# Part of the second feed-forward product by Strassen's seven products

## The chip, the cores and the metric

One Trainium2 chip, one core of it. The metric is the device time of one execution in microseconds (us). The kernel's inputs and outputs are in HBM; the matrix engine (TensorE, PE in the rows), VectorE (DVE), ScalarE (ACT), GpSimd (POOL) and the engine that issues the weight transfers (SP) each take their instructions in order and meet at semaphores.

## The reference, cut to what matters

Two layers (DEPTH = 2) over 640 tokens (128 context, 512 latent) with 1024 channels. A layer normalises, runs three token mixers, projects and gates them ("the mix"), applies an output projection, and then the feed-forward part that this change is about:

```
h2 = rms_norm(x, norm2_g) * (1 + scale2) + shift2
x  = x + gate2 * (square(relu(h2 @ w_ff1)) @ w_ff2)      # 1024 -> 4096 -> 1024, all fp32
```

## The kernel before, in words

**Layout.** Channels lie on the 128 partitions, tokens along the free axis, in two halves of 320 columns. A weight tile is 1024 input channels by 128 output channels, 8 rows of 128x128 (k = 0 to 7). An fp32 product is made from two fp32r parts: ScalarE casts the high part (`cast_entry`, L1278 and L1274), VectorE subtracts it from the full value to get the low part (`low_entry`, L1687), and TensorE does three matmuls (hi*hi, hi*lo, lo*hi) for each row and half. A whole tile takes 8 x 2 x 3 = 48 matmuls of 320 columns.

**Weights.** SP loads tiles in a fixed order into 4 places (`raw`); a place is loaded again when its low parts are made. The high and low parts go through a ring of 4 entries of 4 rows each (`ENTRIES`, `place`). Entry r+4 may be cast when TensorE has used entry r, so the casts stand two tiles or four blocks ahead in ScalarE's and VectorE's queues.

**Feed-forward.** The 4096 hidden channels go in 4 blocks (`FF_BLOCKS`), f = 0 to 3. In a block, 8 hidden tiles are computed (first product), then 8 output tiles from those 8 (second product), each added to `x` with its gate (`add_to_x`, L1885). A hidden tile passes relu and square on ScalarE (L1287, L1289), its cast (L1291, `hid_hi`) and its low part on VectorE (`hid_low`, L1687). `hid` has two buffers, for tile q mod 2, and so has `gqk`, the product before relu.

**Sevens.** Most first products are done in pairs of tiles by Strassen's seven products (`pair_by_sevens`, L894). The 2 x 2 blocks are rows 0 to 3 and 4 to 7 of the weights by the two tiles, and the same rows by the two token halves of h. A pair takes 7 blocks of 4 x 3 = 12 matmuls, 84 for 96. GpSimd makes four sums of weight quarters for it (`block_sums`, L672 to L680; 128x512 each), VectorE combines the results (L1720 to L1732), ScalarE copies three of them (L1300). The four combinations of h are made once, when h is new (`make_diff` L1764, `low_diff`). In block 0 tiles 0 to 3 are whole and 4 to 7 by sevens; in blocks 1 to 3 all are by sevens. The second products are all whole. The pair of tiles q and q+1 is called "pair q" here; the seven blocks, their ring entries and the steps (n) are counted from 0.

**Order.** Each engine's order is written out by hand. In `pair_by_sevens` VectorE does at step n: one result sum, the low part of the entry four ahead, and at some n the low part of a hidden tile. ScalarE does at step n a copy and the cast of the entry four ahead; after step 1 it treats hidden tile q-1, and after step 6 hidden tile q.

**Mix.** The first of 8 mix steps (m = 0) has two whole gate tiles and one whole projection tile, the others use sevens. ScalarE's sigmoids there come ahead of the casts of the next weight tiles.

Of the kernel before, what the change touches and what calls it, by code (L numbers as in the profile page):

```python
# [119 lines left out]

def by_sevens(s):

    i = s % PER
    if MIX0 <= i < OUT0:
        m, q = divmod(i - MIX0, 3)
        return m >= 1 and q < 2
    f, q = divmod(i - FF0, 2 * KT)
    return f >= 0 and q in (range(4, KT) if f == 0 else range(KT))
# [7 lines left out]

def in_mix(s):
    return MIX0 <= s % PER < OUT0


def plain(s):

    return sum(not by_sevens(t) for t in range(s + 1))


def ring_entries():

    out = []
    for s in range(MAIN):
        if leads(s):  # L150
            out += [(s, n, False) for n in range(SEVEN)]
        elif not by_sevens(s):
            out += [(s, n, True) for n in range(2)]
# [4 lines left out]
RING = {s: r for r, (s, n, whole) in enumerate(ENTRIES) if n == 0}  # L158
LEADERS = [s for s in range(MAIN) if leads(s)]
BLOCK = {s: SEVEN * n for n, s in enumerate(LEADERS)}  # L160
# [3 lines left out]
def whole_product(o):  # L164
# [4 lines left out]
    return o < O_FF or not by_sevens(FF0 + o - O_FF)  # L169


def done(o):

    return sum(whole_product(n) for n in range(o + 1)) + (KT if o >= O_MIX else 0)


def blocks_until(s):

    return BLOCK[s] + 6 if leads(s) else BLOCK[s - 1] + 7

# [4 lines left out]
def product_of(s, half):  # L185
# [7 lines left out]
    else:  # L193
        n = done(O_OUT + (i - OUT0))
# [95 lines left out]
def build(nc, xT, cond, first, stream, small, vecs, table, dft, mask, yT, ckvT_out, krT_out, st_out, x_kept):  # L290
# [9 lines left out]
    with ExitStack() as ctx:  # L300
# [143 lines left out]
        p57_sb = sem("p57_sb")  # L444
        mix_sig = sem("mix_sig", 2 * (KT - 1))
# [209 lines left out]
        def _(pool):  # L655
# [6 lines left out]

            def block_sums(s):
# [6 lines left out]
                if b > 0:  # L670
                    pool.wait_ge(block_lo, b - SEVEN + 3)
# [18 lines left out]
            for e.layer in range(DEPTH):  # L690
# [43 lines left out]
        def _(pe):  # L734
# [139 lines left out]
            def pair_by_sevens(o, i, free):  # L874
# [24 lines left out]
                modulation(i + 1)  # L899

# [33 lines left out]
            for e.layer in range(DEPTH):  # L934
# [291 lines left out]
                for f in range(FF_BLOCKS):  # L1226
                    i, o = FF0 + 2 * KT * f, O_FF + 2 * KT * f
                    for q in range(4 if f == 0 else 0):
# [7 lines left out]
                    for q in range(4 if f == 0 else 0, KT, 2):  # L1236
                        n = o + q
                        first = q == (4 if f == 0 else 0)
                        pair_by_sevens(n, i + q, {0: n - 2, 2: n - 1} if first else {0: n - 4, 2: n - 2, 3: n - 1})
# [1124 lines left out]
```

## Time and profile before

| what | value |
|---|---|
| median of 3 runs | 2067.82 us (2067.37 to 2068.98) |
| the profiled execution's own time | 2063.75 us |
| its span, first to last instruction | 2062.0 us |
| mean granted TensorE clock | 0.992 |
| TensorE busy | 1980.4 us, 96% |
| VectorE / ScalarE / GpSimd busy | 59% / 46% / 14% |
| chain that ended last | TensorE 82%, VectorE 11%, ScalarE 3% |

A matmul's row shows its time through the pipeline (309 ns); the next one starts before it ends, so rates are read from start times. "Idle before" is the time an engine sat before an instruction, with what ended it. The chain goes back from the last instruction to what released each step.

### The profile page before, as it was taken

How to read it: one execution, taken by the hardware profiler on the slowest of the kernel's cores; microseconds unless marked ns; L12 is line 12 of the kernel's file. 1: busy time of each engine (PE TensorE's matmuls, PEld its weight loads, DVE VectorE, ACT ScalarE, POOL GpSimd, SP SyncE). 2: the span in 40 equal slices, each digit the busy share in tenths (PEclk: the TensorE clock that was granted, in tenths of full speed). 3: DMA queues.
4: the chain of work that ended last, by engine and by line, in shares of the span. 5: the costliest groups of instructions: out<-in, count | busy, mean ns of one | idle time of the engine just before them, and what ended most of it. 6: DMA issues, size and time to landing. Idle time of an engine off the chain costs nothing.

```text
span 2062.0 us, 34108 instructions
## 1 busy us (share of the span) xinstructions
PE 1980.4 (96%) x13976; PEld 1810.8 (88%) x13976; DVE 1217.4 (59%) x2095; ACT 946.0 (46%) x1746; POOL 284.7 (14%) x229
## 2 busy tenths in 40 slices
PE   6999999999999999999999999999999899999997
PEld 3995688899888999999989866888999899999997
DVE  4245688756468273736553466877664764646464
ACT  5535544534366161625454355453442743535262
POOL 1000000222012130403100000003220312121210
PEclk9999999999999999999999999999999999999999
DMA  9210001343523324242432100113443121213221
GB/s 367 74 51 11 1 27 52 114 166 128 188 81 112 144 91 150 68 149 88 158 109 74 36 6 1 47 58 120 163 162 124 51 89 65 94 62 103 62 94 60
DMA packets 53035, 195.92 MB, mean 95 GB/s; under 512 B 6032, under 2 KB 8144, under 8 KB 52112
## 3 DMA queue, kind: packets, MB, share of 16 engines
q1 hardware_dynamic: 49408, 174.61, 25.2%
q0 software_dynamic: 3472, 19.14, 2.6%
q8 instruction: 111, 1.82, 0.4%
q14 instruction: 44, 0.36, 0.1%
HBM read 187.79 MB, written 5.93 MB: 94 GB/s over the span
## 4 chain that ended last, share of the span: by engine, by line
PE 82%; DVE 11%; ACT 3%; issue 2%; DMA 2%; SPq 0%; ACTq 0%; DVEq 0%
PE ps L742 36%; PE ps L894 23%; PE ps L809 2%; PE ps L914 2%; PE ps L1060 2%; PE ps L923 2%; DVE w_lo_parts L1687 2%; PE ps L760 2%; PE ps L1036 2%; PE ps L847 2%; PE ps L1090 2%; PE ps L1065 1%; ACT scratch L1508 1%; DVE scratch L2095 1%; DVE merged L1764 1%
## 5 line engine op out<-in xcount | busy, mean ns | idle before, releaser
L1687 DVE TENSOR_TENSOR w_lo_parts<-w_raw,w_hi_parts 128x512 fp32r<-128x512 f32 x548 | 403.9, 756 | 242.9 <-ACT w_hi_parts L1274 148.2
L1274 ACT CAST w_hi_parts<-w_raw 128x512 fp32r<-128x512 f32 x296 | 172.1, 619 | 457.5 <-PE ps L742 413.4
L742 PE MATMUL ps<-hid_hi_parts,w_hi_parts 128*128 128x320 f32 x1216 | 280.3, 312 | 2.3 <-DVE merged L2154 1.6
L742 PE MATMUL ps<-hid_lo_parts,w_hi_parts 128*128 128x320 f32 x1216 | 277.0, 309 | 0.0
L742 PE MATMUL ps<-hid_hi_parts,w_lo_parts 128*128 128x320 f32 x1216 | 276.9, 309 | 0.0
L1885 DVE SCALAR_TENSOR_TENSOR x<-ps,modulation,x 128x128 f32<-128x128 f32 (+2 forms) x216 | 81.7, 434 | 319.0 <-PE ps L742 319.0
L742 PEld LDWEIGHTS ps<-hid_hi_parts,w_hi_parts 128*128 128x128 f32 x1216 | 201.9, 188 | 25.3 <-issue 22.1
L1278 ACT CAST w_hi_parts<-w_raw 128x512 fp32r<-128x512 f32 x252 | 152.2, 621 | 137.5 <-PE ps L742 56.7
L742 PEld LDWEIGHTS ps<-hid_lo_parts,w_hi_parts 128*128 128x128 f32 x1216 | 203.3, 188 | 0.0
L742 PEld LDWEIGHTS ps<-hid_hi_parts,w_lo_parts 128*128 128x128 f32 x1216 | 203.3, 188 | 0.0
L894 PE MATMUL ps<-h_hi_parts,w_hi_parts 128*128 128x320 f32 x560 | 173.8, 310 | 0.0
L894 PE MATMUL ps<-h_hi_parts,w_lo_parts 128*128 128x320 f32 x560 | 173.0, 309 | 0.0
L894 PE MATMUL ps<-h_lo_parts,w_hi_parts 128*128 128x320 f32 x560 | 172.7, 309 | 0.0
L894 PE MATMUL ps<-diff_hi_parts_a,w_hi_parts 128*128 128x320 f32 x504 | 156.3, 310 | 7.5 <-DVE w_lo_parts L1687 6.3
L742 PE MATMUL ps<-h_hi_parts,w_hi_parts 128*128 128x320 f32 x640 | 148.6, 313 | 0.0
L742 PE MATMUL ps<-h_hi_parts,w_lo_parts 128*128 128x320 f32 x640 | 145.8, 309 | 0.0
L742 PE MATMUL ps<-h_lo_parts,w_hi_parts 128*128 128x320 f32 x640 | 145.7, 309 | 0.0
L894 PE MATMUL ps<-diff_lo_parts,w_hi_parts 128*128 128x320 f32 x448 | 138.3, 309 | 0.0
L742 PEld LDWEIGHTS ps<-h_hi_parts,w_hi_parts 128*128 128x128 f32 x640 | 106.5, 188 | 11.6 <-issue 10.1
L742 PEld LDWEIGHTS ps<-h_hi_parts,w_lo_parts 128*128 128x128 f32 x640 | 107.0, 188 | 0.0
L742 PEld LDWEIGHTS ps<-h_lo_parts,w_hi_parts 128*128 128x128 f32 x640 | 106.9, 188 | 0.0
L894 PEld LDWEIGHTS ps<-h_hi_parts,w_hi_parts 128*128 128x128 f32 x560 | 105.1, 188 | 1.7 <-issue 1.7
(334 smaller groups left out, 4080.9 us busy)
## 6 DMA issues: line engine op xcount, KB each, us to landing
w_raw<-in_stream SPq DMA_DIRECT2D x312, 512.0 KB, 3.9
scratch<-in_first SPq DMA_DIRECT2D x10, 512.0 KB, 14.3
small_weights<-in_small POOLq DMA_DIRECT2D x2, 2048.0 KB, 10.5
h_scratch<-in_first SPq DMA_DIRECT2D x6, 512.0 KB, 17.3
x<-in_xT POOLq DMA_DIRECT2D x2, 1280.0 KB, 11.8
x<-in_xT POOLq DMA_DIRECT2D x8, 320.0 KB, 4.1
x_kept<-x POOLq DMA_DIRECT2D x8, 320.0 KB, 2.5
x<-x_kept POOLq DMA_DIRECT2D x8, 320.0 KB, 4.1
```

Of the source, the lines that this page charges most:

```text
L742: ins = mm(out[:, h, :], weight(w, s, k), a[:, k, h * HALF:(h + 1) * HALF], start=(first and n == 0), stop=(last and n == 2))
L760: last = mm(pair(o)[:, h, :], weight(w, s, k), a[:, k, half_cols(h)], start=(k == 0 and n == 0), stop=(k == KT - 1 and n == 2))
L809: last = mm(pair(o)[:, h, :], weight(w, s, k), a[:, k, half_cols(h)], start=(k == 0 and n == 0), stop=(k == KT - 1 and n == 2))
L847: last = mm(ps[cols:cols + 32, unit_bank(u), :], cs[:, 2 * j + i, :], tiles[i][:, 4 * P * c:4 * P * (c + 1)], start=(j == 0), stop=(j == U ...
L894: last = mm(ps[:, block_bank(s, n), 0:HALF], place(w, RING[s] + n)[:, k, :], a[:, k, :], start=(n < 4 and k == 0 and c == 0), stop=(k == K ...
L914: last = mm(ps[:, 7 - h, 0:HALF], weight(w, s, k), a[:, k, h * HALF:(h + 1) * HALF], start=(k == 0 and j == 0), stop=(k == KT - 1 and j == 2))
L923: return nc.tensor.transpose(out, src, tab(C_ID))
L1036: last = mm(out, sm[:, w:w + P], cq[:, t, CTX:TOK] if j < 4 else cq[:, t, 0:CTX], start=(t == 0), stop=(t == 1))
L1274: copy(place(wh, r), raw_half(s, n)).then_inc(w_hi, 1)
L1278: copy(place(wh, r), block_source(s, n)).then_inc(block_hi, 1)
L1687: return tt(dst, full, hi.bitcast(F32), ALU.subtract)
L1885: ins = stt(x[:, k, cols], src, modv[:, gate * KT + k, g:g + 1], x[:, k, cols], ALU.mult, ALU.add)
```

## The change

Twelve pairs of second-product tiles are done "by parts": `part_pairs(l, f)` gives pairs 0, 2, 4, 6 for the second layer's blocks 1 and 2, and pairs 0 and 2 for block 3. For block 3 the function does not ask for the layer, so the first layer's block 3 is done so too. In such a pair rows 0 to 3 of the contraction are done by seven products (the 2 x 2 blocks are now rows 0, 1 and rows 2, 3), 7 blocks of 2 x 3 = 6 matmuls; rows 4 to 7 are done whole into the same PSUM banks, 48 matmuls. The pair takes 90 matmuls.

- Four combinations of hidden tiles 0 to 3 are needed. VectorE makes them in `hid_differences` (128x640 each, and one copy) during pairs 2 and 4 of the first product, ScalarE casts them (`cast_hid_diff`) in pairs 4 and 6, VectorE makes their low parts (`low_hid_diff`) in pair 6.
- Since they read the two `hid` buffers, `hid_low(q-1)` moves from step 2 to step 5 in pairs 2 and 4 of these blocks, and ScalarE's square of tile q waits there for `hid_low(q-1)` in place of `hid_low(q-2)`.
- In all pairs by sevens ScalarE treats hidden tile q ahead of the cast of step 6, no longer after it. Tile 7 is treated inside the first pair by parts.
- GpSimd makes four half-size weight sums for each pair by parts (`part_sums`). The result is summed in `gqk`, and VectorE adds it to `x` from there.
- In the second layer block 0 does tiles 4 and 5 whole, and only pair 6 by sevens (`first_seven`).
- In the mix's first step ScalarE's casts come ahead of the sigmoids, and VectorE's low parts of two differences move one product later.

```diff
+def first_seven(l, f):
+    return 0 if f > 0 else 4 if l == 0 else 6
+def part_pairs(l, f):
+    if f == FF_BLOCKS - 1:
+        return range(0, 4, 2)
+    return range(0, KT if l == DEPTH - 1 and f > 0 else 0, 2)
...
+            def part_sums(s):
+                s1, s3 = s1_sb[0][:, 0:2, :], s1_sb[0][:, 2:4, :]
...
+                nc.gpsimd.tensor_tensor(s1, a21, a22, ALU.add).then_inc(part_sum, 1)
+                nc.gpsimd.tensor_tensor(s3, a11, a21, ALU.subtract).then_inc(part_sum, 1)
+                pool.wait_ge(part_lo, PIECES * PART[s] + 1)
...
+            def pair_in_parts(f, q, o):
...
+                block(0, 0, 0)
+                pe.wait_ge(hid_ready, e.at(hid_ready, KT * f + 4))
+                block(1, 0, 2)
+                piece_ready(1)
+                lower(b[1], 1, 0, range(4, 6), False)
+                piece_ready(2)
+                read(n - 2)
+                diff_made(1)
+                block(2, 2, 0)
...
+                block(3, 2, 2)
+                lower(b[1], 1, 0, range(6, KT), False)
+                pe.wait_ge(part_copied, 3 * no + 2)
+                lower(b[2], 1, 1, range(4, KT), False).then_inc(part_mm, 1)
...
             def hid_by_sevens(f, q, o):
...
-                act.wait_ge(hid_ready, e.at(hid_ready, KT * f + q - 1))
+                act.wait_ge(hid_ready, e.at(hid_ready, KT * f + (q if q in (2, 4) and (e.layer, f) in DIFFS else q - 1)))
...
             def pair_by_sevens(f, q, o, first):
                 for n in range(SEVEN):
+                    if n == SEVEN - 1:
+                        hid_by_sevens(f, q, o)
                     pair_step(e.layer * PER + FF0 + 2 * KT * f + q, n)
                     if n == 1 and not first:
                         hid_by_sevens(f, q - 1, o)
-                hid_by_sevens(f, q, o)
+                    if (e.layer, f) in DIFFS and (q, n) in ((4, 4), (4, 5), (6, 4), (6, 5)):
+                        cast_hid_diff(f, {(4, 4): 0, (4, 5): 1, (6, 4): 2, (6, 5): 3}[q, n])
...
+            def hid_differences(f, q, n):
+                b1, b2 = hid[:, :, half_cols(0)], hid[:, :, half_cols(1)]
...
+                if (q, n) == (2, 3):
+                    tt(hid_full(0), b2, b1, ALU.subtract).then_inc(hid_diff, 1)
+                if (q, n) == (2, 4):
+                    e.link(cp(hid_full(1), b2))
+                if (q, n) == (4, 3):
+                    tt(hid_full(1), b2, hid_full(1), ALU.subtract).then_inc(hid_diff, 1)
+                if (q, n) == (4, 4):
+                    tt(hid_full(2), b2, hid_full(0), ALU.subtract).then_inc(hid_diff, 1)
+                if (q, n) == (4, 5):
...
+                    tt(hid_full(3), b1, hid_full(2), ALU.subtract).then_inc(hid_diff, 1)
...
                     if n == 0 and not first:
                         hid_low(f, q - 2)
-                    if n == 2 and not first:
+                    parts = (e.layer, f) in DIFFS
+                    if parts and q in (2, 4):
+                        hid_differences(f, q, n)
+                    if n == (5 if parts and q in (2, 4) else 2) and not first:
                         hid_low(f, q - 1)
+                    if n >= 3 and parts and q == KT - 2:
+                        low_hid_diff(f, n - 3)
...
-                    if m == 0:
-                        first_gate(0)
                     for q in range(2 if m == 0 else 0):
                         act.wait_ge(mm_done, e.at(mm_done, done(o + q)))
+                        split_next(i + q)
+                        if q == 0:
+                            first_gate(0)
                         fn(halves(G[:, 1 + q, :]), pair(o + q), ACT.Sigmoid).then_inc(pair_free[(o + q) % 2], 1)
-                        split_next(i + q)
...
-                            for n in ((1, 2), (3,), ())[b]:
+                            for n in ((1,), (2,), (3,))[b]:
                                 low_diff(True, n)
```

## Rows read from the trace of the kernel before

**Rows 1.** The page, part 1: busy time by engine.

```profile
PE 1980.4 (96%) x13976; PEld 1810.8 (88%) x13976; DVE 1217.4 (59%) x2095; ACT 946.0 (46%) x1746; POOL 284.7 (14%) x229
```

**Rows 2.** Timeline (start us, us, what) of TensorE, layer 2, block 1.

```profile
1731.45 0.31 PE L894 MATMUL ps<-h_hi_parts,w_hi_parts 128*128 128x320 f32 x1
...
1780.72 0.46 PE L742 MATMUL ps<-hid_hi_parts,w_hi_parts 128*128 128x320 f32 x2
```

**Rows 3.** ScalarE's timeline, pair 4: relu, square, cast, weight casts.

```profile
1756.81 0.74 ACT L1287 ACTIVATE gla_q_k<-gla_q_k 128x640 f32<-128x640 f32 x1
1757.58 0.74 ACT L1289 ACTIVATE gla_r<-gla_q_k 128x640 f32<-128x640 f32 x1
1758.35 0.73 ACT L1291 CAST hid_hi_parts<-gla_r 128x640 fp32r<-128x640 f32 x1
...
1759.30 1.14 ACT L1278 CAST w_hi_parts<-w_raw 128x512 fp32r<-128x512 f32 x2
```

**Rows 4.** VectorE's timeline, pairs 4 and 6.

```profile
1742.51 0.48 DVE L1725 TENSOR_TENSOR gla_q_k<-ps,low_rank_latents 128x320 f32<-128x320 f32 x1
...
1757.94 1.70 DVE L1687 TENSOR_TENSOR w_lo_parts<-w_raw,w_hi_parts 128x512 fp32r<-128x512 f32 x1
1759.96 1.40 DVE L1687 TENSOR_TENSOR w_lo_parts<-w_raw,w_hi_parts 128x512 fp32r<-128x512 f32 x1 [0.32 <-ACT w_hi_parts L1278]
...
1762.41 0.68 DVE L1687 TENSOR_TENSOR w_lo_parts<-w_raw,w_hi_parts 128x512 fp32r<-128x512 f32 x1
...
1766.45 1.38 DVE L1687 TENSOR_TENSOR w_lo_parts<-w_raw,w_hi_parts 128x512 fp32r<-128x512 f32 x1 [0.54 <-ACT w_hi_parts L1278]
1767.76 0.48 DVE L1732 TENSOR_TENSOR gla_q_k<-low_rank_latents 128x320 f32<-128x320 f32 x1
```

**Rows 5.** GpSimd's timeline over the same time: the weight sums.

```profile
1742.27 1.48 POOL L680 TENSOR_TENSOR w_raw<-w_raw 128x512 f32<-128x512 f32 x1 [0.80 <-DVE w_lo_parts L1687]
...
1757.79 1.31 POOL L672 TENSOR_TENSOR low_rank_latents<-w_raw 128x512 f32<-128x512 f32 x1 [0.72 <-DVE w_lo_parts L1687]
1759.17 1.63 POOL L674 TENSOR_TENSOR w_raw<-w_raw 128x512 f32<-128x512 f32 x1
1765.99 1.29 POOL L677 TENSOR_TENSOR w_raw<-low_rank_latents,w_raw 128x512 f32<-128x512 f32 x1 [5.19 <-DVE w_lo_parts L1687]
1767.91 1.48 POOL L680 TENSOR_TENSOR w_raw<-w_raw 128x512 f32<-128x512 f32 x1 [0.63 <-DVE w_lo_parts L1687]
```

**Rows 6.** VectorE's timeline after pair 6: the last hidden tile's low part.

```profile
1785.92 0.82 DVE L1687 TENSOR_TENSOR hid_lo_parts<-gla_r,hid_hi_parts 128x640 fp32r<-128x640 f32 x1 [1.35 <-ACT hid_hi_parts L1291]
```

**Rows 7.** VectorE's timeline, layer 2, block 0: two differences of 1280 elements.

```profile
1642.29 5.08 DVE L1764 TENSOR_TENSOR merged<-merged 128x1280 f32<-128x1280 f32 x2
```

**Rows 8.** What TensorE waited for from 1560 to 1660 us.

```profile
PE ps L894 <- DVE w_lo_parts L1687: 4.1, 2, 2.4
PE ps L809 <- DVE h_lo_parts L1844: 2.8, 3, 1.8
PE ps L894 <- DVE diff_lo_parts L1687: 1.2, 1, 1.2
```

**Rows 9.** TensorE's timeline, first pairs of the branch mix, both layers.

```profile
376.29 0.56 PE L742 MATMUL ps<-hid_hi_parts,w_hi_parts 128*128 128x320 f32 x2 [1.58 <-DVE merged L2154]
...
385.46 0.41 PE L894 MATMUL ps<-mix_hi_parts_b,w_hi_parts 128*128 128x320 f32 x1 [1.56 <-DVE w_lo_parts L1687]
...
1403.84 0.41 PE L894 MATMUL ps<-mix_hi_parts_b,w_hi_parts 128*128 128x320 f32 x1 [2.66 <-DVE w_lo_parts L1687]
```

**Rows 10.** ScalarE and VectorE at the start of layer 2's mix.

```profile
1382.37 1.28 ACT L1324 ACT_TABLE_LOAD   x1 [0.99 <-DVEq L2124]
...
1384.90 1.13 ACT L1274 CAST w_hi_parts<-w_raw 128x512 fp32r<-128x512 f32 x2
...
1385.54 1.29 DVE L1687 TENSOR_TENSOR w_lo_parts<-w_raw,w_hi_parts 128x512 fp32r<-128x512 f32 x2 [3.30 <-ACT w_hi_parts L1274]
```

**Rows 11.** Window: length; PE, PEld, DVE, ACT, POOL busy; PEclk, DMA share, GB/s.

```profile
1616.00:1620.00 4.00, 3.03 (x13) 3.03 (x14) 3.13 (x9) 2.94 (x8) 0.00 (x0) 0.70 0.42 135
```

More of the change, by code:

```diff
@@ L134, in leads, with leads_parts, whole_tile @@
     return by_sevens(s) and ((i - MIX0) % 3 == 0 if i < OUT0 else (i - FF0) % 2 == 0)
+def leads_parts(s):
+    return by_parts(s) and (s % PER - FF0) % 2 == 0
 def in_mix(s):
     return MIX0 <= s % PER < OUT0
+def whole_tile(s):
+    return not by_sevens(s) and not by_parts(s)
 def plain(s):
-    return sum(not by_sevens(t) for t in range(s + 1))
+    return sum(whole_tile(t) for t in range(s + 1))
+PIECES = 6
+STEPS = 10
+USED_UP = (2, 5, 4, 7, 8, 10)
 def ring_entries():
@@ L150, in ring_entries, with whole_product @@
         if leads(s):
-            out += [(s, n, False) for n in range(SEVEN)]
-        elif not by_sevens(s):
-            out += [(s, n, True) for n in range(2)]
+            out += [(s, n, "block") for n in range(SEVEN)]
+        elif leads_parts(s):
+            out += [(s, n, "piece") for n in range(PIECES)]
+        elif whole_tile(s):
+            out += [(s, n, "half") for n in range(2)]
     return out
 ENTRIES = ring_entries()
-RING = {s: r for r, (s, n, whole) in enumerate(ENTRIES) if n == 0}
-LEADERS = [s for s in range(MAIN) if leads(s)]
-BLOCK = {s: SEVEN * n for n, s in enumerate(LEADERS)}
+RING = {s: r for r, (s, n, kind) in enumerate(ENTRIES) if n == 0}
+LEADERS = [s for s in range(MAIN) if leads(s) or leads_parts(s)]
+AHEAD = dict(zip(LEADERS[1:], LEADERS))
+BLOCK = {s: SEVEN * n for n, s in enumerate(filter(leads, LEADERS))}
+PART = {s: n for n, s in enumerate(filter(leads_parts, LEADERS))}
 PLAIN = [plain(s) for s in range(MAIN)]
-def whole_product(o):
+def whole_product(o, l):
     if O_MIX <= o < O_OUT:
@@ L193, in product_of @@
     else:
-        n = done(O_OUT + (i - OUT0))
+        n = done(O_OUT + (i - OUT0), l)
     return l * DONE + n
@@ L640, in _ @@
                         sp.wait_ge(block_lo, blocks_until(i))
+                    elif was == "main" and by_parts(i):
+                        sp.wait_ge(part_lo, pieces_until(i))
                     elif was == "main":
@@ L1227, in _ @@
                     i, o = FF0 + 2 * KT * f, O_FF + 2 * KT * f
-                    for q in range(4 if f == 0 else 0):
+                    for q in range(first_seven(e.layer, f)):
                         if q == 0:
@@ L1235, in _ @@
                         modulation(i + q)
[L1236 removed]
+                    for q in range(first_seven(e.layer, f), KT, 2):
                         n = o + q
[L1238 to L1240 removed]
+                        first = q == (first_seven(e.layer, f))
+                        pair_by_sevens(n, i + q, {0: n - 2, 2: n - 1} if first and (e.layer, f - 1) not in DIFFS else {0: n - 3, 2: n - 2, 3: n - 1})
+                    for q in part_pairs(e.layer, f):
+                        pair_in_parts(f, q, o)
+                    for q in whole_second(e.layer, f):
                         tile_ready(i + KT + q)
@@ L1692, in low_entry @@
                     return
-                s, n, whole = ENTRIES[r]
-                if whole:
+                s, n, kind = ENTRIES[r]
+                if kind == "half":
                     dve.wait_ge(w_hi, 2 * PLAIN[s] - 1 + n)
@@ L2187, in _ @@
                     i, o = FF0 + 2 * KT * f, O_FF + 2 * KT * f
-                    for q in range(4 if f == 0 else 0):
+                    for q in range(first_seven(e.layer, f)):
                         split_next(i + q)
```

283 lines of the change are left out of this document (244 added, 39 removed).

## The prediction, made before the changed kernel ran

> **What bounds the kernel now.** I read four views. The page first: TensorE is busy 96% of the span, ScalarE, VectorE and GpSimd far less [rows 1]. Then TensorE's start times: the four pairs by sevens of a block are 4 x 84 = 336 matmuls from 1731.45 to 1780.72, so 49.27 us, 0.1466 us each and no gap [rows 2]. A block of 12 matmuls takes 1.76 us, a pair 12.31, a whole tile 7.04. In the feed-forward blocks TensorE alone sets the pace, so removed matmuls count in full as long as its operands stay ahead. Then the waits of TensorE, for places where they don't: block 0 of layer 2 and the first steps of the mix [rows 8, 9]. Last the timelines of the engines that make the operands [rows 3 to 6]: averages over a layer say that VectorE has room, but the change puts its new work in pairs 2, 4 and 6, and there I have to look.
>
> **What VectorE's timeline shows.** A low part of 512 elements takes 0.68 us (two of them 1.29, so 0.60 from start to start) [rows 4, 10], one of 640 takes 0.82 [rows 6]. But the one begun at 1757.94 takes 1.70: GpSimd's sum runs from 1757.79 to 1759.10, and the low part ends 0.54 later. The next sum, issued at 1759.17, takes 1.63 for 1.30, and the low part of 1759.96 ends 0.56 after it. The same at 1766.45 [rows 4, 5]. So an instruction of VectorE with both inputs in SBUF and one of GpSimd don't run together: one waits until the other is through. A result sum that reads PSUM (1742.51, 0.48 us) runs at full speed inside a GpSimd sum (1742.27 to 1743.75) [rows 4, 5]. Differences pay too: two of 1280 elements took 5.08 us, where 0.82 for 640 gives some 3.1 [rows 6, 7].
>
> The Trainium skill says this as a rule ("SBUF — State Buffer", section "Who interferes with whom"): a VectorE instruction with two SBUF inputs contends with a GpSimd one that reads SBUF, and the loser blocks in full. The trace agrees (1.70 us for 0.68), and by this rule the new differences will block as well.
>
> Per pair by sevens SBUF work is now: seven low parts x 0.60 = 4.2, two hidden low parts x 0.74 (0.82 less what overlaps) = 1.5, L1732 0.4, four sums of GpSimd x 1.30 = 5.2; together 11.3 of 12.31 us. The new work must fit into 1.0 us.
>
> **Part 1, matmuls of the twelve pairs.** 90 for 96, so 12 x 6 x 0.1466 = 10.6 us less.
>
> **Part 2, new waits in the four blocks that feed them.** New on VectorE: one difference and a copy in pair 2 (0.74 + 0.45, the copy an estimate), three differences in pair 4 (2.2), four low parts in pair 6 (3.0). In pair 4 that makes 13.5 us of SBUF work for 12.31. But the order costs more than the sum. I walked the four queues forward in order, with start-to-start times from the rows: ScalarE's relu and square 0.77 each, casts 0.63 (hidden) and 0.52 (weights) [rows 3], copies 0.33 (estimate: half of a 640), VectorE as above with 0.40 for a result sum (0.48 less the overlap), and the exclusion of GpSimd. I chose 0.2 us from a block's last matmul to its reader and 0.1 for other semaphores so that the walk fits the code before. There it gives L1732 at 1767.73 and the last `hid_low` at 1785.88; the rows have 1767.76 and 1785.92 [rows 4, 6], and no wait of TensorE, as in the trace. The same walk of the new code, pair 4, counted from TensorE's start of it (it arrives with ScalarE some 1 us late from pair 2):
>
> - VectorE: `p57` sum ends at 10.5, low part of pair 6's entry 0 at 11.1, difference 1 at 11.8. Now GpSimd's L677 has the port: low part of entry 1 ends at 13.6, L1732 14.0. L680 next: difference 2 ends at 15.9. Result sum 16.3, low part of entry 2 16.9, difference 3 17.7, then the next pair's first sum, so `hid_low(3)` ends at 18.9.
> - ScalarE's square of tile 4 waits for that `hid_low(3)` (it waited for tile 2's before): 19.0 to 19.8, its cast to 20.4, and behind it in the queue the cast of entry 3 to 20.9. Its low part is ready at 21.8.
> - Pair 6's block 3 needs entry 3 at 18.8. TensorE waits 3.0.
>
> In pair 2 the same chain (one difference, copy, `hid_low(1)`, square of tile 2, cast, low part) ends 0.9 late for pair 4. In pair 6, 0.3 for entry 2 and 0.2 for `p57`. The first pair by parts starts (call it 0) with VectorE behind: entry 2 is 0.8 late, the bank of block 3 0.2. Hidden tile 6 gets its relu only at 2.8, its low part stands behind the low part of entry 3 and the fourth difference and is ready at 7.8; without further waits row 6 of the lower product would start at 4.4 + 1.0: 2.4 late. Tile 7 comes at 8.9, row 7 0.7 later than its turn. Before, the last low part was ready 6.0 us after the second product's start (1785.92 + 0.82 - 1780.72) and first used after 42 matmuls, 6.2 us [rows 2, 6]; now it is asked for after 33, 4.8 us.
>
> Sum for a block: 0.9 + 0.3 + 3.0 + 0.2 + 0.8 + 0.2 + 2.4 + 0.7 = 8.5 us, four blocks 34, and 0.3 where a block follows a block by parts. From there on the pairs by parts run free: a pair needs 5.5 low parts, half-size sums of GpSimd (0.65, half of 1.30), and some 5 us of sums and additions in 13.2 us; the cast of entry 5 (its place is free at 7.0, needed at 9.7) has 1.3 us to spare. Bounds per block: if the new instructions didn't exclude GpSimd's, 5.3; if nothing did, 3.3 (the relu chain of tiles 6 and 7 alone); with a few tenths more at each of the nine handovers, 10.5. I take 8.5, since the exclusion stands in the rows for the same kind of instruction. GpSimd's new sums and ScalarE's eight-odd new casts are priced by this walk. SP's loads are still released by low parts a whole pair ahead of their casts.
>
> **Part 3, block 0 of layer 2.** 12 matmuls more, +1.8. TensorE waits there 4.1 + 1.2 = 5.3 us for low parts [rows 8], because the differences of h (5.08 for two) stand ahead of them [rows 7]. With two more whole tiles (14 us) these are made before pair 6 needs them (entries 0 and 1 ready some 5 us early), so -5.3. Net -3.5; bounds -3.5 and +1.8 (nothing saved).
>
> **Part 4, the mix.** ScalarE's casts stood behind a table load, a gate and a sigmoid: 1382.37 to 1384.90, and VectorE sat idle 3.3 us for them [rows 10]. They move some 3 us forward, and one low part of 1.5 us leaves the way of entry 3. The waits of the two first pairs are 1.6 + 1.6 + 2.7 = 5.8 [rows 9]. Walking it, block 3 comes in time and block 4 then waits some 1 us in each layer: -3.5. Bounds 0 and -5.8.
>
> **Sum.** -10.6 + 34.3 + 1.8 - 5.3 - 3.5 = +16.7. The profiled execution took 2063.75 us with a span of 2062.0, so it would be 2080.5; the median of the runs shown lies 4.1 above that execution, and the forecast is against the median: 2067.8 + 16.7 = 2084.5. Within 0.2% (4.1 us) I call it the same.
>
> **Rivals.**
> - A, faster: the differences find gaps. For it, VectorE is busy 59% and ScalarE 46% [rows 1]; against it the 11.3 of 12.31 us. With no new waits the sum is -17.6 (2050.2); it stays faster by over 0.2% as long as a block costs under 3.4 us (-17.6 + 4 x 3.4 = -4.1). The lower bound, no exclusion at all, is 3.3. Likeliest time within it 2060. Chance 0.12.
> - B, the same: the new instructions don't exclude GpSimd's, 5.3 a block: -17.6 + 21.2 = +3.6, 2071. Chance 0.10. Speaks against it: rows 7.
> - C, slower still: the waits lower TensorE's clock. After the waits of 2.8 us ahead of 1617 [rows 8] the granted clock was 0.70 of full speed over a window of 4 us [rows 11], 0.30 x 4 = 1.2 us lost. One or two such falls a block are 4.8 to 9.6 us: 2089 to 2094, 2091 taken. Against it: TensorE works 25 us and more without a gap ahead of the first long wait. Chance 0.13.
> - The forecast, 8 to 9 us a block: 0.65, own range 2077 to 2091.
>
> The change does what it says, and layer 1's block 3 more; were that one not by parts, the sum would be 6.7 lower.
>
> Faster 0.12, same 0.10, slower 0.78. Range for 8 in 10: B's upper part to C's, 2068 to 2095.
>
> **What would show it.** TensorE's waits in the second layer: about 3 us before a matmul of L894 in pair 6 for `w_lo_parts`, about 0.9 in pair 4, and 2.4 + 0.7 in the first pair by parts for `hid_lo_parts`; the same in layer 1's block 3 alone. VectorE's 128x640 differences taking 1.8 to 2 us where a GpSimd sum is under way. No wait in the later pairs by parts. The 5.3 us of layer 2's block 0 gone. Wrong it would be if GpSimd's sums fell elsewhere (they start when low parts end), if VectorE's new instructions passed them, or if the walk misplaced the square of tile 4.

## The result and the profile after

The changed kernel takes 2080.17 us (median of 5 runs, 2077.71 to 2086.09); the kernel before, on the same chip, 2067.82 (5 runs). The ratio is 1.0063, with a 95% interval of 1.0044 to 1.0082: slower. The forecast was 2084.5, with its own range 2077 to 2091.

TensorE has 60 matmuls fewer than in [rows 1] and is busy for as long as before:

```profile
PE 1980.5 (95%) x13916; PEld 1806.5 (87%) x13916; DVE 1287.8 (62%) x2195; ACT 978.6 (47%) x1816; POOL 322.8 (16%) x273
```

The start of the first matmul of each stage in the two profiled executions (spans 2062.0 and 2075.9 us) gives what each part costs.

| stage | before, us | after, us | difference | forecast |
|---|---|---|---|---|
| the mix, layer 1 and layer 2 | | | -3.9, -3.5 | -3.5 for both |
| layer 2, block 0, from its first matmul | 122.1 | 117.4 | -4.7 | -3.5 |
| layer 1, block 3 | 108.1 | 116.0 | +7.9 | +6.7 |
| layer 2, block 1: pairs by sevens; second product | 49.27; 56.34 | 54.47; 55.63 | +4.5 | |
| layer 2, block 2 | 49.27; 56.35 | 54.43; 57.24 | +6.0 | |
| layer 2, block 3, to the last two tiles | 49.27; 42.26 | 55.09; 44.84 | +8.4 | |

The three blocks of layer 2 are +18.9, where 10 pairs at -0.88 and three times 8.5 make +16.7. All rows together are +14.7 (forecast +16.7); the spans differ by 13.9, the medians by 12.4. (An expectation below has +8.3 for layer 1's block 3; that is some 0.4 us too much, since block 0 of that layer differs by 0.4 between the two traces.)

TensorE's timeline in layer 2's block 1, which answers to [rows 2] (the columns as there, at the end the idle time before and what ended it):

```profile
1726.44 0.31 PE L1018 MATMUL ps<-h_hi_parts,w_hi_parts 128*128 128x320 f32 x1
...
1772.23 0.41 PE L1018 MATMUL ps<-diff_hi_parts_a,w_hi_parts 128*128 128x320 f32 x1 [2.83 <-DVE w_lo_parts L1931]
...
1780.91 0.31 PE L1041 MATMUL ps<-hid_hi_parts,w_hi_parts 128*128 128x320 f32 x1
...
1787.32 0.42 PE L1051 MATMUL ps<-hid_hi_parts,w_hi_parts 128*128 128x320 f32 x1 [1.84 <-DVE hid_lo_parts L1931]
...
1788.47 0.42 PE L1051 MATMUL ps<-hid_hi_parts,w_hi_parts 128*128 128x320 f32 x1 [0.44 <-DVE hid_lo_parts L1931]
...
1796.93 0.31 PE L1041 MATMUL ps<-hid_hi_parts,w_hi_parts 128*128 128x320 f32 x1
```

The first wait, 2.8 us, is the one before pair 6's block 3; the other two stand before rows 6 and 7 of the first pair by parts. The pairs by sevens take 54.47 us: 49.27 of work, 2.83 of wait, 2.37 of something else. The first pair by parts takes 16.02 for 13.2; the next begins at 1796.93 and has no wait, nor have the later ones. Block 2 has the same waits (2.81, 1.90, 0.44); each block 3 has them too (layer 1's without the 0.44), with 0.65 more in pair 4.

What makes the 2.8 us, in block 2 of layer 2, where pair 6's block 3 is due at 1879.4. VectorE (answers to [rows 4]):

```profile
1872.41 1.79 DVE L1931 TENSOR_TENSOR w_lo_parts<-w_raw,w_hi_parts 128x512 fp32r<-128x512 f32 x1
...
1874.52 1.91 DVE L1971 TENSOR_TENSOR h_scratch<-gla_r,h_scratch 128x640 f32<-128x640 f32 x1
1876.36 0.48 DVE L2042 TENSOR_TENSOR gla_q_k<-ps,low_rank_latents 128x320 f32<-128x320 f32 x1
...
1877.36 0.81 DVE L1974 TENSOR_TENSOR h_scratch<-gla_r,h_scratch 128x640 f32<-128x640 f32 x1
1878.10 1.35 DVE L1931 TENSOR_TENSOR hid_lo_parts<-gla_r,hid_hi_parts 128x640 fp32r<-128x640 f32 x1
...
1881.59 1.53 DVE L1931 TENSOR_TENSOR w_lo_parts<-w_raw,w_hi_parts 128x512 fp32r<-128x512 f32 x2 [1.74 <-ACT w_hi_parts L1479]
```

GpSimd over the same time (answers to [rows 5]):

```profile
1871.84 1.81 POOL L798 TENSOR_TENSOR w_raw<-low_rank_latents,w_raw 128x512 f32<-128x512 f32 x1 [5.76 <-DVE w_lo_parts L1931]
1874.28 1.48 POOL L801 TENSOR_TENSOR w_raw<-w_raw 128x512 f32<-128x512 f32 x1 [0.63 <-DVE w_lo_parts L1931]
1877.61 1.16 POOL L777 TENSOR_TENSOR low_rank_latents<-w_raw 128x256 f32<-128x256 f32 x1 [1.85 <-DVE w_lo_parts L1931]
```

ScalarE (answers to [rows 3]):

```profile
1876.87 0.74 ACT L1492 ACTIVATE gla_q_k<-gla_q_k 128x640 f32<-128x640 f32 x1 [2.90 <-DVE gla_q_k L2042]
1879.54 0.74 ACT L1494 ACTIVATE gla_r<-gla_q_k 128x640 f32<-128x640 f32 x1 [1.93 <-DVE hid_lo_parts L1931]
1880.31 0.72 ACT L1497 CAST hid_hi_parts<-gla_r 128x640 fp32r<-128x640 f32 x1
1880.94 0.61 ACT L1479 CAST w_hi_parts<-w_raw 128x512 fp32r<-128x512 f32 x1
```

The low part of pair 6's entry 1 takes 1.79 us for 0.68, behind GpSimd's sum that ends at 1873.65. Difference 2 takes 1.91 us where difference 3 takes 0.81: GpSimd's sum lies over it until 1875.76. (Difference 3 began 0.25 us ahead of the next sum, and there it is the sum that takes longer, 1.16 us for 0.74.) The low part of tile 3 takes 1.35 beside the next sum. The square of tile 4 waits for it until 1879.54, and behind its own cast stands the cast of entry 3, which TensorE has wanted since 1879.4. This is the chain of the walk, in its order.

The last two hidden tiles, before the first pair by parts: ScalarE's relus of tiles 6 and 7 and the last cast, and VectorE's low parts (answers to [rows 6]):

```profile
1892.40 0.74 ACT L1492 ACTIVATE gla_q_k<-gla_q_k 128x640 f32<-128x640 f32 x1 [1.73 <-DVE gla_q_k L2042]
...
1895.41 0.73 ACT L1492 ACTIVATE gla_q_k<-gla_q_k 128x640 f32<-128x640 f32 x1
...
1896.95 0.72 ACT L1497 CAST hid_hi_parts<-gla_r 128x640 fp32r<-128x640 f32 x1
```

```profile
1896.57 0.82 DVE L1931 TENSOR_TENSOR hid_lo_parts<-gla_r,hid_hi_parts 128x640 fp32r<-128x640 f32 x1
1897.70 0.82 DVE L1931 TENSOR_TENSOR hid_lo_parts<-gla_r,hid_hi_parts 128x640 fp32r<-128x640 f32 x1 [0.32 <-ACT hid_hi_parts L1497]
```

The second product starts at 1890.97, so the last low part begins 6.7 us after it, where [rows 6] have 5.2 and it is needed at 4.8. ScalarE begins only at 1892.40: VectorE brings the sum that ends tile 6 late.

What the 2.37 us are, again at block 2 of layer 2, in TensorE's timeline and in the windows (length; PE, PEld, DVE, ACT, POOL busy; PEclk, DMA share, GB/s; answers to [rows 11]):

```profile
1882.34 0.64 PE L1018 MATMUL ps<-diff_hi_parts_a,w_hi_parts 128*128 128x320 f32 x1 [2.81 <-DVE w_lo_parts L1931]
...
1883.04 0.47 PE L1018 MATMUL ps<-diff_hi_parts_a,w_lo_parts 128*128 128x320 f32 x1
1883.30 0.47 PE L1018 MATMUL ps<-diff_hi_parts_a,w_hi_parts 128*128 128x320 f32 x1
```

```profile
1880.00:1884.00 4.00, 1.66 (x6) 1.67 (x7) 2.26 (x4) 3.94 (x8) 0.04 (x1) 0.78 0.00 0
1884.00:1888.00 4.00, 4.00 (x24) 4.00 (x23) 2.90 (x6) 2.64 (x6) 0.00 (x0) 0.79 0.39 132
```

Behind the wait the matmuls start 0.26 us apart and not 0.147: the clock is at 1.2 GHz of 2.4. Over the two windows (1 - 0.78) x 4 + (1 - 0.79) x 4 = 1.7 us are lost; some 0.6 more go in the start itself. The trace after has seven such falls in the four blocks (the trace before has none there), three of them behind the 1.8 to 1.9 us wait of the first pair by parts.

The mix ([rows 9]): of the waits for `w_lo_parts` and `merged` none is left in either layer. What TensorE waited for in layer 1, from 355 to 400 us:

```profile
PE ps L866 <- ACT low_rank_latents L1849: 0.2, 1, 0.2
```

ScalarE in layer 2's mix now casts ahead of the table load (answers to [rows 10]):

```profile
1384.46 1.14 ACT L1475 CAST w_hi_parts<-w_raw 128x512 fp32r<-128x512 f32 x2
1385.62 1.28 ACT L1564 ACT_TABLE_LOAD   x1
```

In layer 2's block 0 (1605 to 1700 us) the waits for `w_lo_parts` and `diff_lo_parts` of [rows 8] are gone as well; those of the norm ahead of it stay:

```profile
PE ps L933 <- DVE h_lo_parts L2166: 3.2, 4, 1.8
```

### The profile page after: what moved, and what is told of

It is laid out like the page before. It is cut to its first block, busy times and chain, and to the rows that moved or that the text cites. A ratio compares the mean times of both kernels' runs of the same rounds, so it can differ in the third digit from the quotient of the medians.

```text
span 2075.9 us, 34356 instructions
## 1 busy us (share of the span) xinstructions
PE 1980.5 (95%) x13916; PEld 1806.5 (87%) x13916; DVE 1287.8 (62%) x2195; ACT 978.6 (47%) x1816; POOL 322.8 (16%) x273
## 4 chain that ended last, share of the span: by engine, by line
PE 79%; DVE 12%; ACT 5%; issue 3%; DMA 1%; SPq 1%; ACTq 0%; DVEq 0%
PE ps L866 31%; PE ps L1018 19%; PE ps L1051 4%; PE ps L1041 3%; DVE w_lo_parts L1931 2%; PE ps L1110 2%; PE ps L1256 2%; PE ps L1119 2%; PE ps L884 2%; PE ps L1232 2%; PE ps L971 2%; PE ps L933 2%; PE ps L1286 2%; PE ps L1261 1%; DVE scratch L2417 1%
## 5 line engine op out<-in xcount | busy, mean ns | idle before, releaser
L1931 DVE TENSOR_TENSOR w_lo_parts<-w_raw,w_hi_parts 128x512 fp32r<-128x512 f32 (+1 forms) x558 | 402.3, 741 | 260.4 <-ACT w_hi_parts L1475 147.0
L866 PE MATMUL ps<-hid_hi_parts,w_hi_parts 128*128 128x320 f32 x832 | 192.7, 313 | 0.9 <-issue 0.6
L2207 DVE SCALAR_TENSOR_TENSOR x<-ps,modulation,x 128x128 f32<-128x128 f32 x144 | 54.5, 434 | 221.6 <-PE ps L866 221.6
L866 PE MATMUL ps<-hid_hi_parts,w_lo_parts 128*128 128x320 f32 x832 | 189.5, 309 | 0.0
L866 PE MATMUL ps<-hid_lo_parts,w_hi_parts 128*128 128x320 f32 x832 | 189.5, 309 | 0.0
L1018 PE MATMUL ps<-diff_hi_parts_a,w_hi_parts 128*128 128x320 f32 x492 | 156.3, 318 | 14.9 <-DVE w_lo_parts L1931 14.7
L866 PEld LDWEIGHTS ps<-hid_hi_parts,w_hi_parts 128*128 128x128 f32 x832 | 138.0, 188 | 23.8 <-issue 21.8
L866 PEld LDWEIGHTS ps<-hid_hi_parts,w_lo_parts 128*128 128x128 f32 x832 | 139.1, 188 | 0.0
L866 PEld LDWEIGHTS ps<-hid_lo_parts,w_hi_parts 128*128 128x128 f32 x832 | 139.0, 188 | 0.0
L866 PEld LDWEIGHTS ps<-h_hi_parts,w_hi_parts 128*128 128x128 f32 x672 | 111.8, 188 | 11.6 <-issue 10.9
L1018 PEld LDWEIGHTS ps<-diff_hi_parts_a,w_hi_parts 128*128 128x128 f32 x492 | 94.9, 193 | 19.2 <-DVE w_lo_parts L1931 18.9
## 6 DMA issues: line engine op xcount, KB each, us to landing
small_weights<-in_small POOLq DMA_DIRECT2D x2, 2048.0 KB, 12.4
```

Of the source, the lines that this page charges most:

```text
L866: ins = mm(out[:, h, :], weight(w, s, k), a[:, k, h * HALF:(h + 1) * HALF], start=(first and n == 0), stop=(last and n == 2))
L1018: last = mm(ps[:, block_bank(s, n), 0:HALF], place(w, RING[s] + n)[:, k, :], a[:, k, :], start=(n < 4 and k == 0 and c == 0), stop=(k == K ...
L1931: return tt(dst, full, hi.bitcast(F32), ALU.subtract)
L2207: ins = stt(x[:, k, cols], src, modv[:, gate * KT + k, g:g + 1], x[:, k, cols], ALU.mult, ALU.add)
```

## The experiments

Times are medians. Each ratio is to the kernel before on the same chip in the same session (before: 2066.6, 2068.1 and 2066.6 us in the three sessions).

**No pairs by parts.**

```diff
 def part_pairs(l, f):
-    if f == FF_BLOCKS - 1:
-        return range(0, 4, 2)
-    return range(0, KT if l == DEPTH - 1 and f > 0 else 0, 2)
+    return range(0)
```

> The change with no pair by parts in any block (the mix's order and the seven of block 0 of layer 2 are kept). By the stages of the trace after: 2067.8 - 7.4 (mix) - 4.7 (block 0) = 2055.7 us, with no wait of TensorE over 1 us inside the feed-forward blocks 1 to 3 and no fall of the clock there; the mix is then 3.7 us shorter a layer. By the sizes of the prediction (-3.5 and -3.5) it would be 2060.8. If the parts are not what costs, it stays near 2080.

2056.5 us, ratio 0.9952 (0.9939 to 0.9964). TensorE shows no wait from 1640 to 2020 us, and the clock is at 1.00 there. That is as expected from the stages. The parts are all of the loss, and what else the change does (the mix, block 0, and ScalarE's new order in the pairs by sevens, which this version keeps) gives 10 us together.

**Ten pairs: layer 1's block 3 left whole.**

```diff
-        return range(0, 4, 2)
+        return range(0, 4 if l == DEPTH - 1 else 0, 2)
```

> The change without the pairs by parts of layer 1's block 3 (ten pairs in layer 2 stay). By the stage of the trace after (+8.3 with it) 2080.2 - 8.3 = 2071.9 us; by the prediction's terms (8.5 of waits less two pairs' 1.8) 2073.5. If the cost of the parts lies in layer 2 alone, 2080.

2072.6 us, ratio 1.0031 (1.0019 to 1.0044), 7 us under the whole change (1.0063): within the intervals that block costs what its stage shows, 7.9. The waits of the other blocks stay, but one of them had no fall of the clock behind it, block 3's:

```profile
1987.96 0.41 PE L1018 MATMUL ps<-diff_hi_parts_a,w_hi_parts 128*128 128x320 f32 x1 [2.82 <-DVE w_lo_parts L1931]
1988.21 0.31 PE L1018 MATMUL ps<-diff_lo_parts,w_hi_parts 128*128 128x320 f32 x1
```

**The cast of entry 3 ahead of the square.** ScalarE, pair 4 of the four blocks:

```diff
-                    if n == SEVEN - 1:
+                    late = (e.layer, f) in DIFFS and q in (4,)
+                    if n == SEVEN - 1 and not late:
                         hid_by_sevens(f, q, o)
                     pair_step(e.layer * PER + FF0 + 2 * KT * f + q, n)
+                    if n == SEVEN - 1 and late:
+                        hid_by_sevens(f, q, o)
```

> The whole change; in the four blocks ScalarE casts pair 6's entry 3 ahead of tile 4's relu and square, not behind them. Theory 1 (the cast stands behind a square that waits for VectorE): the cast starts when pair 4's last matmul is through, the low part then stands only behind hid_low(3), the wait before pair 6's block 3 falls from 2.8 us to about 0.9, and the fall of the clock that follows it (1.7 us) goes too: 1.9 + 1.7 = 3.6 a block, 14 in all, 2066 us. Theory 2 (VectorE's own queue is what is late, the cast would have been in time enough): the wait stays over 2 us and the time near 2080. Theory 3 (the clock falls for another reason than the wait): 1.9 a block, 7.6 in all, 2072.6, and the clock falls at the same places.

2080.9 us, ratio 1.0070 (1.0057 to 1.0084): no gain, where the first theory had 14 us. The wait fell nearly as expected, to 1.1 us, and came back in small pieces. What TensorE waited for in block 2 (engine, line, in total, times, longest):

```profile
PE ps L1051 <- DVE hid_lo_parts L1934: 2.6, 2, 2.1
PE ps L1018 <- DVE w_lo_parts L1934: 1.1, 1, 1.1
PE ps L1041 <- DVE w_lo_parts L1934: 0.4, 1, 0.4
PE ps L1018 <- DVE low_rank_latents L2043: 0.4, 1, 0.4
PE ps L1018 <- ACT low_rank_latents L1535: 0.3, 1, 0.3
```

The pairs by sevens take 52.7 us instead of 54.4, but the first pair by parts 18.8 instead of 17.6. In block 2 TensorE now waits at six places instead of three, 4.8 us in all for 5.2. VectorE's order was left as it was, and TensorE, which comes earlier, meets its lateness at other places. My theory named the cast; the cast was only the last link.

**GpSimd's sums made small.**

```diff
+            def columns(s):
+                l, i = divmod(s, PER)
+                n = 2 if i >= FF0 and (l, (i - FF0) // (2 * KT)) in DIFFS else P
+                return lambda *tiles: [t[:, :, 0:n] for t in tiles]
...
-                nc.gpsimd.tensor_tensor(a12, a12, a11, ALU.subtract).then_inc(block_sum, 1)
+                nc.gpsimd.tensor_tensor(*few(a12, a12, a11), ALU.subtract).then_inc(block_sum, 1)
```

(the same on the other seven sums of the two functions)

> The whole change, but GpSimd's weight sums in the four blocks with pairs by parts are made of 2 of 128 columns only; it leaves out the rest of those sums, and every instruction and wait of the other engines stays. Theory 1 (VectorE and GpSimd exclude each other, and this is part of the wait): difference 2 takes 0.82 us instead of 1.91, hid_low(3) 0.82 instead of 1.35, and the wait before pair 6's block 3 is about 0.9 us instead of 2.8; the one before row 6 of the first pair by parts falls by 1.1 from 1.84 to about 0.7. With the clock's falls about 3 to 5 us a block less: 2060 to 2068. Theory 2 (the order of the queues alone makes the wait): 2.8 and 1.84 stay, 2080.

2061.7 us, ratio 0.9970 (0.9960 to 0.9980). Difference 2, and all TensorE's waits of block 2:

```profile
1868.66 0.83 DVE L1978 TENSOR_TENSOR h_scratch<-gla_r,h_scratch 128x640 f32<-128x640 f32 x1
```

```profile
PE ps L1058 <- DVE hid_lo_parts L1938: 2.4, 2, 2.0
```

0.83 for 1.91, and the pairs by sevens are back at 49.3 us in all blocks of layer 2. Without the exclusion nothing is left of the 2.8 us (the expectation had left 0.9 to the order). The time fell into the expected range, but the other half of the theory missed: the wait before row 6 was to fall to 0.7 and is 2.0, with a fall of the clock behind it in each of the four blocks. That wait has another cause, which the prediction had as "the relu chain alone".

**The differences made early.** VectorE's queue in pairs 2 and 4:

```diff
-                if n == 3:
+                if n == 1:
                     dve.wait_ge(hid_sq, e.at(hid_sq, KT * f + q))
-                if (q, n) == (2, 3):
+                if (q, n) == (2, 1):
...
-                if (q, n) == (4, 3):
+                if (q, n) == (4, 1):
...
-                if (q, n) == (4, 4):
+                if (q, n) == (4, 1):
...
-                if (q, n) == (4, 5):
+                if (q, n) == (4, 3):
...
-                    if n == (5 if parts and q in (2, 4) else 2) and not first:
+                    if n == (3 if parts and q in (2, 4) else 2) and not first:
                         hid_low(f, q - 1)
```

> The whole change; VectorE makes the hidden differences as soon as tiles 2 and 3 are squared (two behind step 1 of pair 4, the third and hid_low(3) behind step 3; in pair 2 behind steps 1 and 2), in the gap before GpSimd's sums start, not at steps 3 to 5. Theory 1 (differences beside GpSimd's sums hold back hid_low(3), the square behind it and the cast of entry 3): the wait of 2.8 us ahead of pair 6's block 3 goes, with the clock's fall behind it; the four pairs by sevens take 49.3 to 50 us instead of 54.5. The first pair by parts still takes 16 to 18 us, as in the run with the small sums. Four blocks x 4 to 5 us: 2060 to 2065. Theory 2 (the total of SBUF work in pair 4, 13.5 us for 12.31, is what counts, not its order): the wait comes at another block of the pairs 4 or 6, 2 us and more, time near 2080.

2063.0 us, ratio 0.9981 (0.9972 to 0.9990), 17 us under the change. All three differences of pair 4 run at full speed, and TensorE's only wait in block 2 is the one of the first pair by parts. Two of them run alone; the third begins 0.15 us ahead of a sum of GpSimd, and now the sum is held back:

```profile
1861.64 0.81 DVE L1969 TENSOR_TENSOR h_scratch<-gla_r,h_scratch 128x640 f32<-128x640 f32 x1
1862.38 0.81 DVE L1971 TENSOR_TENSOR h_scratch<-gla_r,h_scratch 128x640 f32<-128x640 f32 x1
...
1864.72 0.81 DVE L1974 TENSOR_TENSOR h_scratch<-gla_r,h_scratch 128x640 f32<-128x640 f32 x1
```

```profile
1864.87 3.56 POOL L798 TENSOR_TENSOR w_raw<-low_rank_latents,w_raw 128x512 f32<-128x512 f32 x1 [5.44 <-DVE w_lo_parts L1931]
```

```profile
PE ps L1051 <- DVE hid_lo_parts L1931: 2.1, 1, 2.1
```

The pairs by sevens take 49.27 to 49.28 us in layer 2. The same instructions, placed in the gap in which GpSimd waits for low parts or just ahead of its sum, cost TensorE no wait there (GpSimd's sum takes 3.56 us for 1.30, and no wait of TensorE follows from it); the sum of SBUF work in pair 4 is no bound. The first pair by parts takes 17.5 to 18.7 us, where the change has 16.0 to 17.6: its wait is 2.1 us for 1.84 to 1.90, with a fall of the clock behind it in each of the four blocks.

**Tile 6's result sum first.** VectorE's queue in pair 6 (cut to its core):

```diff
+                low_hid_diff(f, 0)
...
+                tt(gqk[:, 0, half_cols(1)], ps[:, block_bank(s, 5), 0:HALF], u2, ALU.add).then_inc(pair_free[(o + q) % 2], 1)
+                low_entry(RING[s] + 8)
+                dve.wait_ge(p57_sb, no)
+                tt(gqk[:, 1, half_cols(1)], p57, u2, ALU.add)
+                low_entry(RING[s] + 9)
...
+                low_hid_diff(f, 1)
+                hid_low(f, KT - 2)
+                low_entry(RING[s] + 10)
+                low_hid_diff(f, 2)
```

> The whole change; in pair 6 of the four blocks VectorE makes the result sum that ends tile 6 ahead of the two low parts and the sum p57 + u2, and hid_low(6) and hid_low(7) ahead of the low parts of differences 2 and 3. Theory 1 (the relu chain of tiles 6 and 7 starts late because of VectorE's order): the relu of tile 6 starts some 2 us earlier, the waits of 1.84 and 0.44 before rows 6 and 7 fall to 0 to 0.5, and the first pair by parts takes 13.2 to 14 us instead of 16.0 to 17.6; 2.8 before pair 6's block 3 stays. Four blocks x 3 to 3.5: 2066 to 2068. Theory 2 (ScalarE's six steps relu, square and cast are too long by themselves, whenever they start): over 1.5 us of waits stay in the first pair by parts, 2075 to 2080.

2072.1 us, ratio 1.0021 (1.0012 to 1.0029), 8 us under the change. Block 2:

```profile
PE ps L1018 <- DVE w_lo_parts L1931: 2.8, 1, 2.8
PE ps L1051 <- DVE hid_lo_parts L1931: 1.1, 1, 1.1
```

The first pair by parts takes 14.5 us instead of 16.0 to 17.6: of 2.3 us of waits 1.1 stay, more than expected and less than the rival had. VectorE's order had half of them; this run doesn't show what the other half stands on. The edit also does less than the expectation says: `hid_low(7)` goes ahead of the low part of difference 3 alone, and that of difference 2 still stands before it.

**Both orders.**

> The two orders above together. Theory 1: no wait over 0.5 us and no fall of the clock in the four blocks; what stays of the change is 10.6 less of matmuls, 4.7 in block 0 of layer 2 and 7.4 in the mix: 2045, with 1 us left in waits a block 2049, below the version without pairs by parts (2056.5). If waits move elsewhere as with the cast put first, 2056 to 2065.

2052.5 us, ratio 0.9926 (0.9913 to 0.9938): faster than the kernel before by 15 us and below the version without parts. One wait of 1.3 to 1.4 us a block is left, with no fall of the clock behind it in any of the four; the pairs by sevens take 49.3 us in layer 2, the first pair by parts 14.8 to 15.4. That is more than the expected 2045 to 2049, and the stages say why: the four first pairs are 7.6 us over 13.2 each, and 2045.1 + 7.6 = 2052.7.

```profile
PE ps L1051 <- DVE hid_lo_parts L1931: 1.3, 1, 1.3
```

**Tile 7's relu ahead of two casts, on top of both.** ScalarE:

```diff
                 copy(p5, ps[:, block_bank(s, 2), 0:HALF]).then_inc(part_copied, 1)
+                if q == 0:
+                    cast_entry(r + 3)
+                    cast_hid_diff(f, 3)
```

(they are left out of pair 6's steps 5 and 6, and their low parts follow `hid_low(7)`)

> The two orders together, and in ScalarE's queue around the first pair by parts tile 7's relu, square and cast ahead of the cast of entry 3 and of difference 3 (these two stood before them; on VectorE their low parts follow hid_low(7)). Theory 1 (what is left, 1.35 us ahead of row 7, is ScalarE's queue: 1.15 us of casts ahead of the relus): the wait falls to under 0.3, the first pair by parts takes 13.2 to 13.6 us instead of 14.8 to 15.4, four blocks x 1.5: 6 us under the two orders' 2052.5, so 2046 to 2047. Theory 2 (the casts put back are then late for block 4 or for the copy of P5): a wait of about 1 us at another place of that pair, 2050 to 2053.

2051.8 us, ratio 0.9923 (0.9907 to 0.9939): the same as both orders within the intervals. The wait fell by half, to 0.7 and not to 0.3, and the first pair by parts takes 14.2 to 14.8 us; the 6 us expected are not there (0.6 us in each of four blocks is 2.4, too little for these intervals), and no new wait is either. The trace shows what the rest stands on, in block 2:

```profile
PE ps L1051 <- DVE hid_lo_parts L1936: 0.7, 1, 0.7
```

```profile
1880.95 0.73 ACT L1497 CAST hid_hi_parts<-gla_r 128x640 fp32r<-128x640 f32 x1
1881.68 0.81 DVE L1936 TENSOR_TENSOR h_lo_parts<-h_scratch,hid_hi_parts 128x640 fp32r<-128x640 f32 x1
1882.41 0.81 DVE L1936 TENSOR_TENSOR hid_lo_parts<-gla_r,hid_hi_parts 128x640 fp32r<-128x640 f32 x1
```

Tile 7's cast is done at 1881.68. VectorE then makes the low part of difference 2, which stands first in its order, and `hid_low(7)` begins 0.73 us later; the wait is 0.75. With both orders alone `hid_low(7)` began 0.18 us after its cast, so there ScalarE came last and now VectorE does. That putting `hid_low(7)` ahead would end the wait was not tested.

**The mix and block 0 by themselves.** The kernel before with both parts of the mix's order; with ScalarE's part (`split_next` ahead of `first_gate` and the sigmoid); with VectorE's part:

```diff
-                            for n in ((1, 2), (3,), ())[b]:
+                            for n in ((1,), (2,), (3,))[b]:
                                 low_diff(True, n)
```

and the change with neither parts nor the mix's order, which leaves `first_seven` and ScalarE's order in the pairs by sevens.

> The kernel before with the change's order of the mix alone (casts of the weights ahead of the gate's and the mix's sigmoids, one low part a step). By the stages of the two traces 7.4 us less (3.7 a layer): 2059 to 2060. By the prediction's term 3.5 us less: 2063. If the stages' difference is the noise of two executions, 2066.

> The kernel before with only ScalarE's part of the mix's order: the casts of the weights ahead of the gate's and the mix's sigmoids. The mix's two parts together gave -8.1 us. Theory 1 (the cast of the weights is what the 1.6 us waits of the first pair stand on): two of the waits of a layer go, 2 x 1.6 x 2 layers = 6.4 less, and the 2.7 of the low part of entry 3 stays in part: 2061 to 2062. Theory 2 (low parts of the differences alone are what is late): 2067.

> The kernel before with only VectorE's part of the mix's order: one low part of a difference a step instead of two, one, none. Theory 1: entry 3's low part comes 1.5 us sooner, one wait of a layer falls by that: 3 us less in two layers, 2065. If both parts are needed together, no change, 2067 to 2068.

> The change with neither the mix's order nor any pair by parts: only pairs 6 and 7 of layer 2's block 0 by sevens, 4 and 5 whole. From the stages of the traces -4.6 us (12 matmuls more, the waits of 5.3 us for low parts gone, with some 1 us of restart behind them): 2063.3. By the prediction's term -3.5: 2064.4. From the difference of the runs without parts (-9.9) and with the mix alone (-8.1), -1.8: 2066.

| version | us | ratio | interval |
|---|---|---|---|
| mix, both parts | 2059.5 | 0.9961 | 0.9948 to 0.9973 |
| mix, ScalarE's casts | 2059.7 | 0.9965 | 0.9954 to 0.9975 |
| mix, VectorE's low parts | 2064.6 | 0.9989 | 0.9977 to 1.0001 |
| block 0 | 2063.9 | 0.9987 | 0.9976 to 0.9997 |

The casts alone give -7.2 us, both parts -8.1, and the low parts -2.3, an interval that holds nothing too: the two act in part on the same waits. (The expectation for the casts counts two waits of 1.6 in each layer; the trace before has them in layer 1 alone, and one of 2.7 in layer 2.) With the low parts alone the wait of 1.6 for `merged` is there in both layers, and one of 0.7 for `w_lo_parts`. With the casts alone TensorE still waited from 355 to 400 us for

```profile
PE ps L894 <- DVE w_lo_parts L1687: 0.5, 1, 0.5
PE ps L742 <- ACT low_rank_latents L1609: 0.2, 1, 0.2
```

Block 0 gives -2.7 (-5.0 to -0.6): the interval holds both -4.7 and -3.5 and does not tell them apart.

## Why the prediction came out

**Right: the sign, and the mechanism of the 2.8 us.** Difference 2 and the low part of tile 3 blocked by GpSimd's sums, the square of tile 4 behind them, the cast of entry 3 behind the square: the walk had 3.0 us, the trace 2.8, and the sums made small took it to zero, as did the differences made early. [Rows 7] told rightly that differences are held back too: 1.91 us measured for 0.81. Rival B (5.3 a block, same) falls with it, and so does A: the gaps were there, as the early differences show, but the changed code did not use them. The rule that the prediction took from the Trainium skill (page "SBUF — State Buffer", section "Who interferes with whom") is that a VectorE instruction with two SBUF inputs and a GpSimd one that reads SBUF contend. The traces agree: 1.91 us begun behind a sum, 0.81 to 0.83 without one, beside one cut to 2 columns, or begun ahead of it.

**Right: the relu chain of tiles 6 and 7.** 2.4 + 0.7 in the prediction, 1.84 + 0.44 in the trace, still there with the sums made small, and halved when VectorE's order was mended. The size came near partly by luck. Counted from the second product's start, the walk had tile 6's relu at 2.8, its low part ready at 7.8 and row 6 due at 5.4; in block 2 they are 1.4, 6.4 and 4.4. All three came 1.0 to 1.4 us sooner than the walk had it, and the difference nearly stayed.

**Too large: the small terms of part 2.** Of 0.9 (pair 4), 0.3, 0.2, 0.8 and 0.2 only the first exists, 0.65 us, and only in the two blocks 3. One reason fits: in blocks 1 and 2 of layer 2 the change casts and lowers only half of tiles 0 and 1 (`hid_cols`), where the walk took 0.74 us for each low part everywhere. VectorE's timeline of block 2 has

```profile
1853.04 0.48 DVE L1931 TENSOR_TENSOR hid_lo_parts<-gla_r,hid_hi_parts 128x320 fp32r<-128x320 f32 x1
```

That this is the cause was not tested. So the waits of a block are 5.1 to 5.8 us where the sum had 8.5.

**Left out: what a wait costs beyond itself.** That is rival C's mechanism, which I gave 0.13 because TensorE works 25 us without a gap ahead of the first wait. The falls came all the same, one or two a block at 1.7 us, with that long stretch of work ahead of them. The rival's own price of 1.2 us was too small: it reads one window of [rows 11], and the next one, 1620 to 1624, stands at 0.87, which makes 1.7 together. The bound of 3.3 us without any exclusion was too low for the same reason: with the sums made small a block still cost 4.1 to 4.7. Waits, starts and falls together cost 8.0, 9.6, 10.2 and 9.8 us in the four blocks, 37.6 in all against 34.3 forecast: block by block the size was near because the two errors cancel, not because the walk was exact.

**Mis-sized: part 4, the mix.** -3.5 forecast, -7.4 by the stages and -8.1 (0.9961) by its own run. All the waits of [rows 9] went, 5.8 us, which was the term's upper bound, and about 0.8 a layer beyond their length. The wait of 1 us before block 4, with which the walk made -5.8 into -3.5, doesn't exist.

**Part 3, block 0.** The 5.3 us of waits went as the term says. The stage gives 1.2 more, what follows such waits; the separate run can't confirm that.

Summed: -10.6 + 37.6 - 4.7 - 7.4 = +14.9, for a forecast of +16.7 (the table has +14.7, since some 0.2 of the 9.8 stood in the kernel before too). The range held, near its middle; part 2 was 3.3 dearer than forecast, and parts 3 and 4 were 1.2 and 3.9 cheaper, so the terms were further off than the sum.

## What to carry to other kernels

Count more than the work against the time of a step: see where in the step the other user of SBUF runs. The same three differences cost 4 to 5 us a block beside GpSimd's sums, and TensorE did not wait for them when they stood 4 to 6 us earlier in the same queue. When a wait has a chain behind it, mend its first link: bringing only the last one forward (the cast) spread the same lateness over six places. And test parts of a change apart: here the two that looked minor gave 10 us, the main one lost them until its queue was put in order.

## What the runs showed of the hardware

- TensorE's clock fell behind short waits in the midst of steady work. In the blocks with pairs by parts of the change and of the seven versions that have them, 24 waits of 2.0 to 2.8 us had a fall of 1.7 us behind them 23 times (the run with ten pairs shows the exception), six of 1.84 to 1.90 us three times, sixteen of 0.7 to 1.4 us never. What decides between the cases is not settled by these runs; the row at 1987.96 shows that the length of the wait alone does not.
- A wait costs more than its length even where the clock stays: with ten pairs, block 3's pairs by sevens took 53.86 us for 49.27 of work and 3.47 of waits, so 1.1 us more for two waits; with both orders, 14.81 for 13.2 and 1.34, so 0.3 for one.
- Who begins first passes, and the other pays. In each of the four blocks of the change, difference 1 began some 0.2 us ahead of a sum of GpSimd and took 0.82 us, and the sum took 1.8 for 1.30; difference 2 began some 0.2 us behind a sum and took 1.91.
- A copy of VectorE from SBUF to SBUF in float32 (L1967) was held back beside GpSimd's sum as the differences were: 1.57 us in all four blocks of the change, 0.49 with the differences made early, where no sum lies beside it (the estimate had 0.45):

```profile
1860.44 1.57 DVE L1967 COPY h_scratch<-gla_r 128x640 f32<-128x640 f32 x1
```
